# RWKV input projection in pieces of one PSUM bank, with memory attention and RWKV preparation as steps between the pieces

## The reference

```python
u = rms_norm_2(x, mix_norm[0])
proj = u @ a_w_in                      # 256 x 2816 = 2560 shifted columns + 256 memory queries
p = token_shift(proj[:, :2560], mu)    # p + mu * (previous token's p - p)
r, k, v, w_lo, a_lo, g_lo = split(p)   # 768, 768, 768, 64, 64, 128 columns
w_log = -softplus(-(w0 + tanh(w_lo) @ w_up)) - 0.5
decay = exp(-exp(w_log))
a = sigmoid(a0 + a_lo @ a_up)
g = sigmoid(g_lo) @ g_up
kk = k * kk_scale;  kk = kk / max(norm_per_head(kk), 1e-12)
k = k * (1.0 + (a - 1.0) * k_a)
y = rwkv7_scan(r, decay, k, v, kk, a)  # 12 heads of 64, then a norm per head, a bonus, the gate g
q = rms_norm_2(proj[:, 2560:])         # 4 heads of 64
y_mem = softmax(q @ k_mem.T / 8) @ v_mem   # 256 memory rows, k_mem and v_mem made earlier
x = x + concat(y, y_mem) @ a_w_out
```

## Time and profile before

| | |
|---|---|
| median of 3 runs | 2065.04 us (2063.79 to 2066.41) |
| the profiled execution's own time | 2066.67 us |
| its span, first to last instruction | 2064.5 us |
| TensorE, matmuls | 1919.6 us busy (93%) |
| VectorE | 1175.4 us busy (57%) |
| ScalarE | 943.0 us busy (46%) |
| mean granted TensorE clock | 0.974 of full speed |

### The profile page before, as it was taken

One profiled execution on the slowest core, in us unless ns is written; L12 is line 12 of the kernel. 1 busy time (PEld: TensorE's weight loads), 2 busy tenths in 40 slices (PEclk: granted clock), 3 DMA queues, 4 the chain that ended last, 5 costly groups with the idle time before them and its releaser, 6 DMA issues.

```text
span 2064.5 us, 32699 instructions
## 1 busy us (share of the span) xinstructions
PE 1919.6 (93%) x13840; PEld 1405.1 (68%) x13840; DVE 1175.4 (57%) x1627; ACT 943.0 (46%) x1344; POOL 75.9 (4%) x129
## 2 busy tenths in 40 slices
PE   6999988898988987889999999899999999999999
PEld 4777523234976331348889977788887888778887
DVE  5677733445877333446566454666565676536555
ACT  4344444345364443454445543354445454445442
POOL 2041000000010000000000000000000000200000
PEclk9999998999999999999999979999999999999999
DMA  9887999998957999986555300065554655605553
GB/s 353 298 286 265 336 387 385 387 367 282 341 166 286 362 387 387 370 293 209 184 192 177 120 1 4 31 216 184 190 195 151 208 185 195 175 3 184 189 198 103
DMA packets 261346, 476.42 MB, mean 231 GB/s; under 512 B 8513, under 2 KB 118145, under 8 KB 255825
## 3 DMA queue, kind: packets, MB, share of 16 engines
q1 hardware_dynamic: 251264, 431.81, 60.0%
q0 software_dynamic: 9936, 42.52, 6.0%
HBM read 472.16 MB, written 2.14 MB: 230 GB/s over the span
## 4 chain that ended last, share of the span: by engine, by line
PE 75%; DMA 12%; DVE 6%; ACT 4%; issue 2%; SPq 1%; POOL 0%; ACTq 0%; DVEq 0%; POOLq 0%
PE psum L1153 16%; PE psum L1188 11%; PE psum L1596 9%; PE psum L1158 8%; PE psum L1108 6%; DMA experts<-in_exp_w_down 5%; DMA experts<-in_exp_w_up 3%; DMA experts<-in_exp_w_gate 2%; PE psum L1099 2%; PE psum L1100 1%; PE psum L1101 1%; PE psum L1538 1%; PE psum L1324 1%; PE psum L1057 1%; PE psum L1121 1%
## 5 line engine op out<-in xcount | busy, mean ns | idle before, releaser
L2964 DVE TENSOR_TENSOR w_lo<-ring,w_hi 128x2048 fp32r<-128x2048 f32 x191 | 436.1, 2289 | 180.8 <-ACT w_hi L2249 179.4
L2249 ACT ACTIVATE w_hi<-ring 128x2048 fp32r<-128x2048 f32 x191 | 364.8, 1914 | 219.6 <-PE psum L1188 118.4
L1153 PE MATMUL psum<-h_both,w_hi 128*128 128x512 f32 x1408 | 442.9, 396 | 1.9 <-DVE h_both L3705 1.3
L1158 PEld LDWEIGHTS psum<-h_both,w_lo 128*128 128x128 f32 x1408 | 264.7, 188 | 61.7
L2455 ACT ACTIVATE pool<-experts 128x512 f32 x332 | 183.8, 620 | 225.9 <-PE psum L1596 98.1
L3404 DVE COPY pool<-experts 128x512 f32 x380 | 141.0, 423 | 242.9 <-PE psum L1596 114.7
L1158 PE MATMUL psum<-h_both,w_lo 128*128 128x256 f32 x1408 | 277.7, 278 | 0.0
L1153 PEld LDWEIGHTS psum<-h_both,w_hi 128*128 128x128 f32 x1408 | 217.5, 189 | 5.6 <-issue 1.7
L2281 ACT ACTIVATE pool<-psum 128x512 f32<-128x512 f32 x88 | 52.6, 598 | 254.5 <-PE psum L1158 254.5
L1596 PE MATMUL psum<-pool 128*32 128x512 f32 x1008 | 127.7, 621 | 13.2 <-DVE pool L3404 8.4
L1596 PE MATMUL psum<-experts,pool 128*32 128x512 f32 x1024 | 123.2, 610 | 17.8 <-DMA experts<-in_exp_w_down 15.1
(11 more groups left out here) (476 smaller groups left out, 2979.2 us busy)
## 6 DMA issues: line engine op xcount, KB each, us to landing
experts<-in_exp_w_gate SPq DMA_DIRECT2D x64, 1024.0 KB, 12.2
experts<-in_exp_w_up SPq DMA_DIRECT2D x64, 1024.0 KB, 14.3
experts<-in_exp_w_down SPq DMA_DIRECT2D x64, 1024.0 KB, 15.0
ring<-in_ffn_pre_w_in SPq DMA_DIRECT2D x44, 1024.0 KB, 5.1
ring<-in_ffn_post_w_in SPq DMA_DIRECT2D x44, 1024.0 KB, 5.1
ring<-in_ada_w SPq DMA_DIRECT2D x24, 1024.0 KB, 6.9
ring<-in_ffn_pre_w_out SPq DMA_DIRECT2D x22, 1024.0 KB, 4.9
ring<-in_ffn_post_w_out SPq DMA_DIRECT2D x22, 1024.0 KB, 4.9
```

The lines of the kernel that those rows point to most:

```text
L1153: pe.matmul(bank(4 + 2 * j + f).rearrange("p (s n) -> p s n", s=2), wh[:, k, P * f:P * f + P], h_both[:, :, k, :], start=k == 0, stop=Fals ...
L1158: return pe.matmul(bank(4 + 2 * j + f)[:, 0:T], wl[:, k, P * f:P * f + P], h_hi[:, k, :], start=False, stop=k == KD - 1, skip_group_check= ...
L2249: act.activation(w_hi[:, (s["split"] + r) % 3, :], piece(s["pieces"][r]), ACT.Copy)\
L2964: dve.tensor_tensor(w_lo[:, slot, :], piece(s["pieces"][r]), w_hi[:, slot, :].bitcast(F32), ALU.subtract).then_inc(sem("w_lo"), 1)
```

## The change

The projection's pieces are handled one by one, each in one PSUM bank of three (`a_bank`: 2, 0, 1 in turn). `A_FIRST` gives their order by first tile: queries (20), decay, a and gate inputs (18), keys (6, 8, 10), values (12, 14, 16), receptance (0, 2, 4). After every piece each engine has its steps of the preparation and of the memory attention: `beside_a(n)` on TensorE, and the branches on n in the loops of ScalarE and VectorE. All `warm` matmuls of this stretch and `before_values` are removed. The attention uses one buffer of each kind (banks 4 and 5 for scores, 6 for turned probabilities, 3 for outputs; `mem_p`, `mem_pt`). What stays behind the last piece: two value products, one turn, `rw_v`, `rw_kk`, bonus, `rw_b`, `rw_k`. The up-projections go to `early_hid` (`low_up`, `gate_up`) on GpSimd's queue, ahead of `c_reset`, after the feed-forward block `pre0`; on SP's queue the masks now come ahead of the lnx rows. The product of receptance and `e_down` and that for the bonus are made in parts of two tiles (`queries_scaled`). In the end VectorE waits for `rwkv_in` ahead of the chunk phase, and TensorE for it and for the last attention output. Left out below, and in the kernel as it was: the two sigmoid and gate helpers, the key factors (n = 5, ScalarE), the key products (n = 6, VectorE) and the two-column value sums (n = 9, TensorE, where one line of "..." stands).

```diff
+A_FIRST = [20, 18, 6, 8, 10, 12, 14, 16, 0, 2, 4]
...
-                self.add("gemm", (name, o + lo, cols, k0, ks), ("w_lo", self.split))
+                at = P * A_FIRST[len(g["pieces"]) - 1] if name == "a_in" else o + lo
+                self.add("gemm", (name, at, cols, k0, ks), ("w_lo", self.split))
...
+                    for o, src in ((3072, a["c_rw_masks"]), (1536, a["a_lnx_g_2"][0].partition_broadcast(P)),
+                                   (2304, a["a_lnx_b_2"][0].partition_broadcast(P))):
+                        sp.dma_start(rwkv_par[:, o:o + src.shape[1]], src).then_inc(sem("rwkv_in"), 16)
...
+            pl.wait_ge(sem("x_new"), X_NEW["pre0"])
+            pl.dma_start(low_up[0:64], a["a_w_up_2"][0]).then_inc(sem("cols_in"), 16)
+            pl.dma_start(low_up[64:P], a["a_a_up_2"][0]).then_inc(sem("cols_in"), 16)
+            pl.dma_start(gate_up, a["a_g_up_2"][0]).then_inc(sem("cols_in"), 16)
             pl.wait_ge(sem("norm_T"), 8 * (NORMS.index("n_mix0") + 1))
             pl.dma_start(rw_reset, a["c_reset"]).then_inc(sem("route_in"), 16)
...
+            def a_piece(n):
+                g = PL.gemms["a_in"]
+                pe.wait_ge(sem("w_lo"), g["split"] + n + 1)
+                if n == 3:
+                    for e in moved("a_in", 5):
+                        pe.wait_ge(sem(e[0]), e[1])
+                elif n > 3:
+                    pe.wait_ge(sem("shift_mixed"), 2 * (n - 3))
+                wh, wl = (w[:, (g["split"] + n) % 3, :].rearrange("p (k n) -> p k n", k=KD) for w in (w_hi, w_lo))
+                o = bank(a_bank(n))
...
+            def mem_scores(j):
+                pe.wait_ge(sem("att_exp"), JOB_BASE["mem0"] + j)
+                for e, (sg,) in enumerate(job(*JOBS["mem0"][j])[0]):
+                    pe.matmul(bank(4 + e)[:, 0:T], sg["q"], sg["k"], start=True, stop=True).then_inc(sem("att_scores"), 1)
+            def mem_turn(j):
+                J = JOB_BASE["mem0"] + j
+                pe.wait_ge(sem("att_exp"), J + 1)
+                pe.wait_ge(sem("att_pts"), J)
+                for k in range(4):
+                    m = pe.transpose(bank(6)[:, P * k:P * k + P], mem_p[:, k // 2, P * (k % 2):P * (k % 2) + P], ident)
+                m.then_inc(sem("att_pt"), 1)
+            def mem_values(j):
+                J = JOB_BASE["mem0"] + j
+                pe.wait_ge(sem("att_pts"), J + 1)
+                pe.wait_ge(sem("att_o"), J)
+                for e, (sg,) in enumerate(job(*JOBS["mem0"][j])[0]):
+                    for kt in range(NT):
+                        m = pe.matmul(bank(3)[:, 64 * e:64 * e + 64], mem_pt[:, P * (2 * e + kt):P * (2 * e + kt) + P], sg["v"][kt],
+                                      start=kt == 0, stop=kt == NT - 1)
+                m.then_inc(sem("att_pv"), 1)
+            def beside_a(n):
+                if n == 2:
+                    transposes("mem0_q", ("heads_ok", 3))
+                    pe.wait_ge(sem("cols_in"), 112)
+                    pe.wait_ge(sem("rw_inputs"), RW_IN["decay_low"])
+                    low_products(range(4), LOW_W_BANKS, LOW_A_BANKS)
+                elif n == 3:
+                    transposed("mem0_q")
+                    pe.wait_ge(sem("rw_inputs"), RW_IN["a_first"])
+                    low_products(range(4, 6), LOW_W_BANKS, LOW_A_BANKS)
+                    pe.wait_ge(sem("rw_inputs"), RW_IN["gate_low"])
+                    gate_products(range(4))
+                elif n == 4:
+                    gate_products(range(4, 6))
+                elif n == 5:
+                    pe.wait_ge(sem("rw_inputs"), RW_IN["a_last"])
+                    pe.wait_ge(sem("rw_inputs"), RW_IN["squares_2"])
+                    key_sums()
+                elif n == 6:
+                    pe.wait_ge(sem("rw_gate"), 2)
+                    pe.wait_ge(sem("rw_inputs"), RW_IN["key_root"])
+                    key_norms()
+                    pe.wait_ge(sem("mem_in"), 32)
+                    mem_scores(0)
+                elif n == 7:
+                    pe.wait_ge(sem("rw_ss"), 3)
+                    mem_turn(0)
+                    mem_scores(1)
+                elif n in (8, 9):
+                    mem_values(n - 8)
+                    mem_turn(n - 7)
+                    mem_scores(n - 6)
+                if n == 9:
+                    pe.wait_ge(sem("shift_mixed"), 14)
...
+                    m.then_inc(sem("rw_ss_ps"), 1)
+            for n in range(len(A_FIRST)):
+                a_piece(n)
+                beside_a(n)
+            mem_values(2)
+            mem_turn(3)
             pe.wait_ge(sem("rw_ss"), 4)
             transposes("rw_v", ("rw_scaled", 1))
+            mem_values(3)
             transposes("rw_kk")
...
             transposes("rw_b", ("rw_scaled", 2))
-            transposes("rw_k", ("rw_scaled", 3))
+            transposes("rw_k", ("rw_scaled", 3), ("rw_dec", 3))
             pe.wait_ge(sem("rw_scaled"), 4)
+            pe.wait_ge(sem("att_o"), 12)
+            pe.wait_ge(sem("rwkv_in"), 48)
+            par = rwkv_par
             transposed("rw_k")
...
+            g_a = PL.gemms["a_in"]
+            split_piece("a_in", 2, 2)
+            for n in range(len(A_FIRST)):
+                act.wait_ge(sem("w_used"), g_a["split"] + n + 1)
+                if n == 0:
+                    act.activation(flat(q_mem_a), bank(a_bank(0)), ACT.Copy).then_inc(sem("ev_act"), 1)
+                else:
+                    shifted(n)
+                if n == 1:
+                    act.wait_ge(sem("shift_mixed"), 2)
+                    act.activation(F[0:64, 18, :], F[0:64, 18, :], ACT.Tanh).then_inc(sem("rw_inputs"), 1)
+                    act.activation(F[:, 19, :], F[:, 19, :], ACT.Sigmoid).then_inc(sem("rw_inputs"), 1)
+                elif n == 2:
+                    transposes("mem0_q")
+                    act.wait_ge(sem("rw_up_ps"), 2)
+                    low_sigmoids(W[0], LOW_W_BANKS, range(4), 20)
+                    low_sigmoids(W[1], LOW_A_BANKS, range(4), 26)
+                    key_squares(0)
+                elif n == 3:
+                    act.wait_ge(sem("rw_up_ps"), 4)
+                    low_sigmoids(W[0], LOW_W_BANKS, range(4, 6), 20)
+                    low_sigmoids(W[1], LOW_A_BANKS, range(4, 6), 26)
+                    act.wait_ge(sem("rw_up_ps"), 5)
+                    gate_moved(range(2))
+                    key_squares(1)
+                elif n == 4:
+                    key_squares(2)
+                    act.wait_ge(sem("rw_up_ps"), 6)
+                    gate_moved(range(2, 3))
+                elif n == 5:
+                    act.wait_ge(sem("rw_inputs"), RW_IN["a_last"])
+                    act.wait_ge(sem("rw_ss_ps"), 1)
...
+                    m.then_inc(sem("rw_inputs"), 1)
+                    act.wait_ge(sem("rw_ss"), 2)
+                    act.activation(key_norm, key_norm, ACT.Sqrt).then_inc(sem("rw_inputs"), 1)
+                elif n == 6:
                     act.wait_ge(sem("rw_prepared"), 1)
                     act.activation(Wf[0], Wf[0], ACT.Exp, scale=-DECAY).then_inc(sem("rw_dec"), 1)
...
+                    mem_exp(0)
+                elif 7 <= n <= 9:
+                    if n == 7:
+                        act.activation(e_up, Wf[2], ACT.Exp, scale=DECAY).then_inc(sem("rw_dec"), 1)
+                    mem_turned(n - 7)
+                    mem_exp(n - 6)
+                if n + 3 < len(A_FIRST):
+                    split_piece("a_in", n + 3, n + 3)
+                if n == 0:
+                    heads(3)
+                if n == 7:
                     act.activation(flat(e_down), Wf[2], ACT.Exp, scale=-DECAY).then_inc(sem("rw_dec"), 1)
...
+            mem_turned(3)
...
+            def queries_scaled(n):
+                pair = slice(A_FIRST[n], A_FIRST[n] + 2)
+                dve.wait_ge(sem("shift_mixed"), 2 * n)
+                dve.wait_ge(sem("rw_dec"), 3)
+                step(dve.tensor_tensor(flat(Fr[:, pair, :]), flat(Fr[:, pair, :]), flat(e_down[:, pair, :]), ALU.mult))
+                return dve.tensor_tensor(flat(W[4][:, pair, :]), flat(Fr[:, pair, :]), flat(Fk[:, pair, :]), ALU.mult)
+            g_a = PL.gemms["a_in"]
+            split_piece("a_in", 1, 1)
+            split_piece("a_in", 2, 2)
+            for n in range(len(A_FIRST)):
+                if n == 0:
+                    for e in moved("a_in", 5):
+                        dve.wait_ge(sem(e[0]), e[1])
+                    heads_stats(3, mq, 64)
+                else:
+                    shifted(n)
+                if n == 7:
+                    mem_max(1)
+                elif n == 8:
+                    mem_out(0)
+                    mem_max(2)
+                elif n == 9:
+                    mem_out(1)
+                    mem_max(3)
+                if n == 3:
+                    dve.wait_ge(sem("route_in"), 48)
+                    dve.wait_ge(sem("rw_inputs"), RW_IN["w_first"])
+                    scans(range(4))
+                elif n == 4:
```

(54 more changed lines are left out.)

272 lines of the change are left out of this document (103 added, 169 removed).

## The result

| | before | after |
|---|---|---|
| median of the runs (range, runs) | 2064.41 us (2060.95 to 2066.41, 4) | 2047.41 us (2046.31 to 2048.82, 4) |
| profiled execution, own time / span | 2066.67 / 2064.5 us | 2048.82 / 2046.9 us |
| first product of the first piece | 1113.56 us | 1115.92 us |
| first product of the chunk phase | 1235.02 us | 1217.59 us |
| the stage between the two | 121.46 us | 101.67 us |

The account below looks back on a forecast made before the run. Bound: a TensorE latency chain of 57.87 us behind the projection. It becomes 33.0, gaining 24.9; less waits 2.5 and handovers 2.1 gives 20.3, less clock 6.5 gives 13.8. Forecast 2052 us, range 2043 to 2061.

Parts of the forecast that it names:

- steps between pieces, at full clock: TensorE's preparation and attention steps placed between projection pieces, priced without waits at full clock: 20.3 us.
- tail, at full clock: TensorE work left behind the last piece, up to the chunk phase, without waits at full clock: 12.7 us.
- handovers from engine to engine: Cost beyond durations of a dozen handovers on the chain after the key sums, plus rounding: 2.1 us.
- TensorE waits between pieces: Behind piece 9, the value product waits 1.7 us for VectorE's output and the turn 0.8: 2.5 us.
- clock behind piece 6: No loss forecast here: the granted clock was to be 1.00 to piece 9.
- clock behind piece 9, with piece 10: Waits, turn and two-column sums behind piece 9 drop the clock; slower sums and piece 10's start cost 3.5 us.
- clock in the tail: Clock falls behind the last piece as before: 2.5 us for the transposes, 0.5 for bonus sums, together 3.
- The overlap: Preparation and attention run between pieces: 57.87 us becomes 33.0 without waits at full clock, a gain of 24.9 us.
- signs that I named for being wrong: A stall behind piece 2, a wait for a low split ahead of a piece, or piece 7, 8 or 9 at half clock.
- The moved loads: Three up-projection loads moved to GpSimd's queue cost nothing; if late, TensorE stands behind piece 2 for a few us.
- The clock holds: Rival: piece 10 restores the clock at once and centring carries the tail; gain 20, time 2045; chance 0.18.
- Side engines become the bound: Rival: VectorE and ScalarE set the pace between pieces 6 and 10; waits 8 to 10 us, time 2059; chance 0.17.

Follow-up runs that it names:

- after_again: The changed kernel unaltered, run a second time; stage 101.4 us, median 2045.6 us, ratio to before 0.9904.
- steps_behind: Changed kernel with all preparation and attention steps moved behind the eleventh piece on all three engines; stage 128.7 us, median 2076.9 us, ratio to before 1.006.
- attention_behind_b: Changed kernel with only the memory attention moved behind the last piece on all three engines; stage 110.5 us, median 2059.4 us, ratio to before 0.9976.
- sums_spread: Changed kernel with the 24 two-column value sums split into eight behind each of pieces 7, 8 and 9; stage 101.6 us, ratio to before 0.9908.
- spread_128b: Changed kernel with value sums spread behind pieces 7, 8, 9 and key norms over 128 rows; stage 98.5 us, median 2044.2 us, ratio to before 0.9896.
- norms_128b: Changed kernel with key norms multiplied over 128 rows, 116 of them zeros, instead of 12; stage 101.7 us, ratio to before 0.9906.
- dve_more_b: Changed kernel with two extra unused VectorE products (3.5 us) in turn 7; stage 108.3 us, median 2053.1 us, ratio to before 0.9945.
- spread_128_dve: Changed kernel with spread value sums, key norms over 128 rows and two extra VectorE products in turn 7; stage 104.7 us, ratio to before 0.9948.
- spread_128_again: Second run of the changed kernel with spread value sums and key norms over 128 rows; stage 96.8 us, median 2046.4 us, ratio to before 0.992.

## Why the prediction came out right, and where its numbers were off

The forecast was 2052 us with 2043 to 2061, and the time was 2047.4. The mechanism and the place of the main loss were as predicted. The size was not: the forecast has a gain of 13.8 us in the stage, and it was 19.8. The terms can be read off the chain of waits of after:

| term | predicted | measured |
|---|---|---|
| steps between pieces, at full clock | 20.3 | 19.8 |
| tail, at full clock | 12.7 | 12.3 |
| handovers from engine to engine | 2.1 | 0 |
| restart of a piece behind a step | 0 | 1.4 |
| TensorE waits between pieces | 2.5 | 0.2 |
| clock behind piece 6 | 0 | 1.5 |
| clock behind piece 9, with piece 10 | 3.5 | 3.1 |
| clock in the tail | 3 | 0 |
| sum, against 57.9 and 58.1 before | 44.1 | 38.3 |

The steps: 89.35 us from the start (1115.92) to the end of piece 10 (1205.27), less 68.24 in the pieces, are 21.1; of these the clock made 1.1 (scores 1.15 instead of 0.63, sums 3.20 instead of 2.58), and 0.2 is the turn at 1192.34 (0.64 instead of 0.45). The pieces: 68.24 - 11 x 5.76 = 4.9, of which piece 7 has 1.0 (6.94 - 5.95), piece 10 has 2.5 (8.46 - 5.95), and 1.4 is the rest, some 0.2 for each of the eight pieces that follow a step. The tail is 1217.59 - 1205.27 = 12.32. The clock's rows hold for this trace: in after_again the two falls cost about 3 and 1.5 us, the other way round.

**The overlap** was right to 1 us (steps and tail, 32.1 for 33.0), and steps_behind and attention_behind_b show it by taking it away. It was well founded because every term had a row, at full clock or halved from one at half clock.

**The handovers** were luck. The 2.1 us stood for the ways between the engines, and none of these lies on TensorE's path between the pieces. What came in their place, 1.4 us of restarts, is not in the prediction at all.

**The clock in the tail** is the largest error, 3 us of the 6. The step read "the same order of work comes as before (...), so I take the same fall". It did not fall in any of three traces of the kernel after. Twelve transposes, 24 two-column sums and 24 transposes, 6.6 us of work of which the Trainium skill ("TensorE: Matmul & The Clock Gate", Part 4) has the transposes not count as busy the same way, ran at 1.00; the last 24 took 2.69 us instead of 5.24. The measurement decides, but it does not turn the rule round: in sums_spread, spread_128b, steps_behind and attention_behind_b the clock fell in the tail too, and in each of the four chains of waits the 24 transposes took 4.36 us. Over all eleven traces with the new order of work they ran at full clock in seven and in part at half clock in four. What decides it is not shown. That TensorE comes to this work from piece 10 is not enough, since it did so in sums_spread and spread_128b too. One row of a fall was not enough to price the next one; a half-and-half value of 1.5 us would have been the better choice.

**The waits** were predicted at 2.5 us behind piece 9. The chain names none, and there are 0.2. VectorE's and ScalarE's results were in time by nothing: the third job's probabilities end and the turn that reads them starts at the same moment, 1192.3, as the timeline of after shows (the weights of this turn, PEld, are loaded only then):

```profile
1192.07 0.20 ACT L2686 ACTIVATION_READ_ACCUMULATOR pool<-psum,tiny 128x1 f32 x1
1192.16 0.83 ACT L2657 ACTIVATE pool<-psum,rcols 128x255 f32<-128x255 f32 x2
1192.32 0.42 PEld L1807 LDWEIGHTS psum<-keep,pool 128*128 128x128 f32 x4
```

I had the third probabilities at 77.1 us after the start, and they came at 76.4; I had TensorE asking at 76.3, after a wait of 1.7 us for VectorE, and it asked at 76.3 without that wait, because 1.5 us of clock and over 1 of restarts had made it late. norms_128b takes that clock loss out, and waits of 1.0 and 0.5 us are there at once, at the place and from the engines that the prediction names. So its step on the waits was right as a mechanism; it left out that a loss ahead of them is not added to them.

**The fall behind piece 6** was not forecast ("1.00 to piece 9"), and a piece 7 at half clock was one of the signs that I named for being wrong: it was so for 2.3 of its 6.9 us here, and for 5.3 us in after_again. It came in five of five traces with the key norms over 12 rows and four scores behind them, and in none of four with the norms over 128 rows. By norms_128b it cost nothing in the end. So the forecast took the clock's fall for a matter of two-column matmuls, transposes and pauses, and this one came without any of them.

**The clock behind piece 9** was right in place and size: 3.1 us for 3.5, and back 5.8 us after piece 10 began (1196.8 to about 1202.6) where I took 5.4.

**The rest.** The moved loads cost nothing, as said: there is no wait at piece 2 or for a low split ahead of a piece. "The clock holds" (2045) is nearest in time, but it is not what happened: 4.6 us went to the clock, and the forecast's waits did not come on top. The forecast's own span for the chunk phase, 1221, became 1217.6, in a run which began the stage 2.4 us late. "Side engines become the bound" was near in another sense: dve_more_b shows that 3.5 us more on VectorE would have cost 6.7, and the time would have been 2053.

## What to carry to other kernels

Where a latency chain over three engines stands behind a dense phase, put its steps between pieces of the dense phase; price each step at full clock from rows, and add about 0.2 us for each return to the pieces (as here). Then compare the two chains, the dense engine's and the side engines', at each place where they meet, since a loss in one is free as long as the other is later, and losses of both are not added. The slack there is worth keeping: a delay of 3.5 us cost 6.7, because the pause also took the clock with it.

## What the runs showed of the hardware

- TensorE was busy 3.00 of 3.00 us in 1166 to 1169 and again in 1169 to 1172, and yet was granted 0.52 in the second. That was behind 12 products over 12 rows and four over 64, and it came in five of five traces. With 116 zero rows added, the same products (2.7 and 2.8 us) left it at 1.00, in four of four traces. With 12 rows and a full piece right behind them it held as well, in the one trace of attention_behind_b, so the 12 rows alone did not do it there. What else it takes is open.
- A pause of 2.8 us with 0.5 more shortly after it was followed by 10 us at half clock, in spite of pieces of 5.76 us of dense work before it and behind it (spread_128_dve); with 2.9 and 0.5 it was 14 us (dve_more_b).
- A fall lasted from 3.4 us (behind piece 6) to 14 (dve_more_b), and behind piece 6 it had 3.4 or 6.8 us in one and the same kernel (after, after_again); the length of one is no constant.
- The tail is on an edge: the clock held over it in one trace and fell in the other of one and the same kernel (spread_128_again and spread_128b). Such a term wants a value between.
